# Two norms behind an MLP folded into the next projection's input and eviction, and the squares of the norm before it taken group by group

## What is computed

```python
# end of first_block
h2 = modulate(rmsnorm(x, norm2_g), sh2, sc2)            # h * (1 + sc2) + sh2
x = x + gt2 * (square(relu(h2 @ w_mlp_in)) @ w_mlp_out)  # 2048 -> 8192 -> 2048
x = rmsnorm(x, final_norm_g)
# start of second_block
h = rms_norm(x, norm_mix_pre)
u = h @ w_in                                             # 2048 -> 4352
...                                                      # convolutions and pooling on u, then @ w_out
x = x + rms_norm(y, norm_mix_post)                       # x here is the output of the first block
```

## Time and profile before

| | |
|---|---|
| median of 3 runs | 2858.72 us (2858.38 to 2859.18) |
| the profiled execution, its own time | 2861.59 us |
| its span, first to last instruction | 2859.5 us |
| mean granted TensorE clock in it | 0.969 |
| TensorE busy | 2675.6 us, 94% |
| VectorE busy | 1665.1 us, 58% |
| ScalarE busy | 1158.2 us, 41% |

### The profile page before, as it was taken

The page is one execution under the profiler, slowest core; times in us unless marked ns, Lnnn a source line. Parts: engine busy times, 40 slices in busy tenths (PEclk is TensorE's granted clock), DMA queues, the critical chain, the costliest instruction groups (busy, mean ns, idle before and its releaser), DMA issues.

```text
span 2859.5 us, 45648 instructions
## 1 busy us (share of the span) xinstructions
PE 2675.6 (94%) x20456; PEld 2552.4 (89%) x20456; DVE 1665.1 (58%) x1955; ACT 1158.2 (41%) x1266; POOL 10.6 (0%) x23
## 2 busy tenths in 40 slices
PE   6899999999989999999999799849699999999996
PEld 3488898899989999999999699839599999999996
DVE  4266666387767545455454457954566546654664
ACT  3222555343335434344343343323444434443442
POOL 0000000000000000000000000000000000000000
PEclk9899999999999999999999899969799999999998
DMA  9766565487765655555555244415155555555451
GB/s 375 306 234 229 199 220 192 162 297 273 293 235 215 225 180 184 186 179 190 177 185 184 103 148 154 153 51 188 55 181 181 188 181 188 177 186 183 177 192 45
DMA packets 76211, 546.91 MB, mean 191 GB/s; under 512 B 8720, under 2 KB 8848, under 8 KB 11120
## 3 DMA queue, kind: packets, MB, share of 16 engines
q1 hardware_dynamic: 73424, 533.53, 51.5%
q0 software_dynamic: 2304, 9.96, 0.9%
q10 hardware_dynamic: 288, 0.50, 0.1%
HBM read 538.72 MB, written 5.24 MB: 190 GB/s over the span
## 4 chain that ended last, share of the span: by engine, by line
PE 86%; DVE 8%; DMA 2%; ACT 2%; issue 1%; SPq 0%; POOL 0%; ACTq 0%; DVEq 0%
PE acc L264 24%; PE acc L266 24%; PE acc L268 24%; DVE cacc L1178 2%; PE mp L450 2%; DVE wlo L232 2%; DMA raw<-in_w_mod 2%; PE acc L284 2%; PE acc L285 1%; PE acc L286 1%; PE mp L286 1%; PE mp L284 1%; PE mp L285 1%; PE mp L333 1%; DVE macc L377 1%
## 5 line engine op out<-in xcount | busy, mean ns | idle before, releaser
L232 DVE TENSOR_TENSOR wlo<-raw,whi 128x1024 fp32r<-128x1024 f32 x813 | 984.2, 1223 | 875.3 <-ACT whi L222 873.1
L222 ACT ACTIVATE whi<-raw 128x1024 fp32r<-128x1024 f32 x813 | 853.6, 1058 | 1347.7 <-PE acc L268 1153.4
L264 PE MATMUL acc<-hh,whi 128*128 128x256 f32 x3616 | 1034.5, 286 | 37.0 <-issue 23.7
L266 PE MATMUL acc<-hl,whi 128*128 128x256 f32 x3616 | 1025.6, 284 | 0.0
L268 PE MATMUL acc<-hh,wlo 128*128 128x256 f32 x3616 | 1025.4, 284 | 0.0
L264 PEld LDWEIGHTS acc<-hh,whi 128*128 128x128 f32 x3616 | 695.9, 192 | 48.9 <-issue 39.2
L266 PEld LDWEIGHTS acc<-hl,whi 128*128 128x128 f32 x3616 | 696.2, 193 | 1.2 <-issue 1.0
L268 PEld LDWEIGHTS acc<-hh,wlo 128*128 128x128 f32 x3616 | 695.8, 192 | 0.0
L264 PE MATMUL acc<-mh,whi 128*128 128x256 f32 x2240 | 631.4, 282 | 16.5 <-DVE ml L1262 15.1
L268 PE MATMUL acc<-mh,wlo 128*128 128x256 f32 x2240 | 633.6, 283 | 0.0
L266 PE MATMUL acc<-ml,whi 128*128 128x256 f32 x2240 | 633.6, 283 | 0.0
(11 more groups left out here) (242 smaller groups left out, 1706.6 us busy)
## 6 DMA issues: line engine op xcount, KB each, us to landing
raw<-in_w_in SPq DMA_DIRECT2D x98, 1024.0 KB, 4.8
raw<-in_w_mod SPq DMA_DIRECT2D x96, 1024.0 KB, 5.0
raw<-in_w_up SPq DMA_DIRECT2D x88, 1024.0 KB, 4.8
raw<-in_w_mlp_in SPq DMA_DIRECT2D x64, 1024.0 KB, 4.8
raw<-in_w_mlp_out SPq DMA_DIRECT2D x64, 1024.0 KB, 4.7
raw<-in_w_down SPq DMA_DIRECT2D x44, 1024.0 KB, 4.7
raw<-in_w_out SPq DMA_DIRECT2D x32, 1024.0 KB, 4.8
raw<-in_w_fourier_out SPq DMA_DIRECT2D x8, 1024.0 KB, 4.9
```

Of the source, the lines that this page charges most:

```text
L222: nc.scalar.activation(whi[:, r, :], raw_slot(k)[:, 2 * GC * j:2 * GC * (j + 1)], ACT.Copy)\
L232: nc.vector.tensor_tensor(wlo[:, r, :], raw_slot(k)[:, 2 * GC * j:2 * GC * (j + 1)], whi[:, r, :].bitcast(f32), ALU.subtract).then_inc(S[" ...
L264: nc.tensor.matmul(dst, whi[:, r, cols], hi[:, kt, :], start=begin, stop=False, skip_group_check=True)
L266: nc.tensor.matmul(dst, whi[:, r, cols], lo[:, kt, :], start=False, stop=False, skip_group_check=True)
```

## The change

**norm2.** The squares of quad g are taken behind the eviction of output group g, by ScalarE. VectorE adds the squares of quads 1 and 2 onto those of quad 0, one addition each in groups 2 and 3 (`x2_add`). TensorE sums that total (four matmuls) and behind it the squares of quad 3 (four more). The jobs of the apply are five: two of two tiles, then three of four (`N2_JOBS`), and TensorE waits for them piece by piece (`n2_ready`).

**The two norms behind the MLP.** With f the final norm's weight, m the mix norm's, r1 and r2 the factors per token, h is x * (f * m) * (r1 * r2), and the mean square that r2 needs is r1 * r1 * mean((x * f)^2). So ScalarE writes `hh` as x scaled by `gg` = f * m behind the eviction of each output group of the last MLP chunk, VectorE writes `hl` (`mix_lo`), both without the factors; ScalarE takes the squares of x and of x * f of the same quad (`mix_quad`), VectorE adds them up (`mix_sums`). TensorE goes from the MLP's last group into `w_in_2`, and does the two sums by ones, eight matmuls, in front of the fourth quad of channel tiles of its first group (`u_ready`). Both roots are taken during that group, and r1 * r2 goes in at the eviction of every group of `w_in_2` (`mix_evict`, in place of the copies). x itself gets its f * r1 later, 16 instructions spread over groups 2 to 4.

Removed: `norm_squares`, `norm_root`, `norm_sums`, `norm_rstd` of three norms (2, 3 and 4), L1140, L1143, the four jobs behind them. The other norms are only renumbered. The diff, cut to its core:

```diff
@@ helpers
+        N2_JOBS = [(0, 2), (2, 2), (4, 4), (8, 4), (12, 4)]
+        LO_MIX = 8 + len(N2_JOBS)
+        def ones_sum(pe, dst, part, begin, end):
+            for t in range(4):
+                last = nc.tensor.matmul(dst, ones[:, :], part[:, t * NT:(t + 1) * NT],
+                                        start=begin and t == 0, stop=end and t == 3)
+            return last
...
@@ scalar
             for g in range(0, 4):
                 C(st)
-            all_read(act, F_OUT)
-            norm_squares(act, 2, xT2)
-            norm_root(act, 2, mp[0])
+                i = 1 - g % 2
+                act.wait_ge(acc_free[i], F_FILL[i] + 6 + g // 2 + 1)
+                if g >= 2:
+                    act.wait_ge(S["x2_add"], g - 1)
+                nc.scalar.activation(tiles(tmp[:, min(g, 1), :]), xT2[:, 4 * g:4 * g + 4, :], ACT.Square)\
+                    .then_inc(S["x2_sq"], 1)
+            act.wait_ge(S["x2_ps"], 1)
+            nc.scalar.activation(root[:, :], mp[0][:, 0:NT], ACT.Sqrt, bias=eps[:, 0:1], scale=1.0 / D)\
+                .then_inc(S["x2_rt"], 1)
...
+            act.wait_ge(S["lo_ok"], LO_MIX)
+            def mix_quad(g):
+                act.wait_ge(acc_free[g % 2], F_MLP[g % 2] - 1 + g // 2)
+                for t in range(4):
+                    kt = 4 * g + t
+                    last = nc.scalar.activation(hh[:, kt, :], xT2[:, kt, :], ACT.Copy, scale=gg[:, kt:kt + 1])
+                last.then_inc(S["u_hi"], 1)
+                if g >= 2:
+                    act.wait_ge(S["x4_add"], 2 * g - 2)
+                nc.scalar.activation(tiles(tmp[:, min(g, 1), :]), xT2[:, 4 * g:4 * g + 4, :], ACT.Square)
+                for t in range(4):
+                    kt = 4 * g + t
+                    last = nc.scalar.activation((sqb if g else stage)[:, t * NT:(t + 1) * NT], xT2[:, kt, :],
+                                                ACT.Square, scale=pcol("final_norm_g", kt))
+                last.then_inc(S["x4_sq"], 1)
...
                 for g in range(4):
                     C(st)
-            all_read(act, F_MLP)
...
+                    if c == MLP_CHUNKS - 1:
+                        mix_quad(g)
+            C(st, 6)
+            act.wait_ge(S["x4_ps"], 1)
+            nc.scalar.activation(root[:, :], mp[0][:, 0:NT], ACT.Sqrt, bias=eps[:, 0:1], scale=1.0 / D)\
+                .then_inc(S["x4_rt"], 1)
+            act.wait_ge(S["x4_s"], 1)
+            nc.scalar.activation(root[:, :], tmp[:, 1, 0:NT], ACT.Sqrt, bias=eps[:, 0:1], scale=1.0 / D)\
+                .then_inc(S["x4_rt"], 1)
+            C(st, 2)
+            for b in range(3):
+                C(st)
@@ vector
             for g in range(4):
                 if g:
-                    C()
+                    C(2)
+                    if g >= 2:
+                        sum_add("x2_add", "x2_sq", g - 1, tmp[:, 0, :], tmp[:, 1, :])
+                    C(6)
...
+            dve.wait_ge(S["x2_rt"], 1)
+            own(nc.vector.reciprocal(rstd[:, 0, :], root[:, :]))
+            apply_dve(dve, 8, 0, [(xT2, hh, hl, a, n) for a, n in N2_JOBS])
+            def mix_lo(g):
+                dve.wait_ge(S["u_hi"], g + 1)
+                for t in range(4):
+                    kt = 4 * g + t
+                    last = nc.vector.scalar_tensor_tensor(hl[:, kt, :], xT2[:, kt, :], gg[:, kt:kt + 1],
+                                                          hh[:, kt, :].bitcast(f32), ALU.mult, ALU.subtract)
+                last.then_inc(S["u_lo"], 1)
+            def mix_sums(g):
+                if g:
+                    sum_add("x4_add", "x4_sq", g, tmp[:, 0, :], tmp[:, 1, :])
+                    sum_add("x4_add", "x4_sq", g, stage[:, :], sqb)
...
+                    if c == MLP_CHUNKS - 1 and g:
+                        C(2)
+                        mix_lo(g - 1)
+                        C(2)
+                        mix_sums(g - 1)
+                        C(4)
...
-            norm_rstd(dve, 3)
...
+            C(1)
+            mix_lo(3)
+            C(1)
+            mix_sums(3)
+            C(4)
+            dve.wait_ge(S["x4_rt"], 1)
+            own(nc.vector.reciprocal(rstd[:, 0, :], root[:, :]))
+            own(nc.vector.tensor_tensor(tmp[:, 1, 0:NT], mp[0][:, GC:GC + NT], rstd[:, 0, :], ALU.mult))
+            nc.vector.tensor_tensor(tmp[:, 1, 0:NT], tmp[:, 1, 0:NT], rstd[:, 0, :], ALU.mult)\
+                .then_inc(S["x4_s"], 1)
+            dve.wait_ge(S["x4_rt"], 2)
+            own(nc.vector.reciprocal(rstd[:, 1, :], root[:, :]))
+            own(nc.vector.tensor_tensor(rstd[:, 1, :], rstd[:, 1, :], rstd[:, 0, :], ALU.mult))
+            C(2)
+            def mix_evict(i, dst, n=4):
+                group_done(dve, st)
+                nc.vector.tensor_tensor(dst, tiles(acc[i][:, 0:n * NT]), rbc(1, n), ALU.mult)\
+                    .then_inc(acc_free[i], 1)
...
+                    if g + b:
+                        C(4)
+                        for kt in range(16 * (2 * g + b - 1) // 3, 16 * (2 * g + b) // 3):
+                            nc.vector.scalar_tensor_tensor(xT2[:, kt, :], xT2[:, kt, :], pcol("final_norm_g", kt),
+                                                           rstd[:, 0, :], ALU.mult, ALU.mult).then_inc(S["x1_ok"], 1)
+                        C(4)
+                    mix_evict(b, uT[:, 3 * TA + 8 * g + 4 * b:3 * TA + 8 * g + 4 * b + 4, :])
@@ tensor
-            norm_sums(pe, 2, mp[0])
+            pe.wait_ge(S["x2_add"], 2)
+            ones_sum(pe, mp[0][:, 0:NT], tmp[:, 0, :], True, False)
+            pe.wait_ge(S["x2_sq"], 4)
+            ones_sum(pe, mp[0][:, 0:NT], tmp[:, 1, :], False, True).then_inc(S["x2_ps"], 1)
+            def n2_ready(k0):
+                pe.wait_ge(S["lo_ok"], 9 + (k0 // 2 if k0 < 4 else 1 + k0 // 4))
...
-            norm_sums(pe, 3, mp[0])
-            pe.wait_ge(S["rt_ok"], 4)
-            norm_sums(pe, 4, mp[0])
+            def u_ready(q):
+                pe.wait_ge(S["u_lo"], q + 1)
+                if q == 3:
+                    pe.wait_ge(S["x4_add"], 6)
+                    ones_sum(pe, mp[0][:, 0:NT], tmp[:, 0, :], True, True)
+                    ones_sum(pe, mp[0][:, GC:GC + NT], stage[:, :], True, True).then_inc(S["x4_ps"], 1)
```

More of the change, by code:

```diff
@@ L178, in build @@
             st_ok sm_ok dec_ok o_ok oss_ok ort_ok ons_ok oT_ps ot_ok ohi_ok olo_ok p_ps p_sb y_ps yhi_ok ylo_ok
+            x2_sq x2_add x2_ps x2_rt gg_ok u_hi u_lo x4_sq x4_add x4_ps x4_rt x4_s r1_ok x1_ok
             mt_ok mhi_ok mlo_ok x_back relu_ok rsq_ok hhi_ok hid_ok
@@ L295, in acc_wait, with mm_feature @@
             st.f[i] += evictions
-        def mm_feature(pe, st, i, hi, lo, frees, nkt=KT, w=GC, ready=None, free=None):
+        def mm_feature(pe, st, i, hi, lo, frees, nkt=KT, w=GC, ready=None, free=None, each=None):
             if free:
@@ L306, in mm_feature @@
                     ready(k0 // 4)
+                if each:
+                    each(k0)
                 feature_piece(pe, st, i, hi, lo, k0, nkt, w)
@@ L504, in apply_act @@
                     act.wait_ge(S["lo_ok"], n - 1)
-                for t in range(4):
-                    kt = 4 * q + t
+                for t in range(cnt):
+                    kt = a + t
                     part = tmp[:, n % 2, t * NT:(t + 1) * NT]
@@ L511, in apply_act @@
                 act.wait_ge(S["t2_ok"], n + 1)
-                nc.scalar.activation(hi[:, 4 * q:4 * q + 4, :], tiles(tmp[:, n % 2, :]), ACT.Copy)\
+                nc.scalar.activation(hi[:, a:a + cnt, :], tiles(tmp[:, n % 2, 0:cnt * NT]), ACT.Copy)\
                     .then_inc(S["hi_ok"], 1)
@@ L830, in _ @@
             all_read(act, F_OUT2)
[L831 to L837, removed]
+            norm_squares(act, 2, yT)
+            norm_root(act, 2, mp[0])
+            act.wait_ge(S["vt_ok"], 4)
+            norm_squares(act, 3, xT2)
+            norm_root(act, 3, mp[0])
+            apply_act(act, LO_MIX, [(hh, None, lambda kt: pcol("norm_ffn_pre_2", kt), None, 4 * q, 4)
+                                    for q in range(4)])
+            act.wait_ge(S["lo_ok"], LO_MIX + 4)
             def ffn_pair(st, c, p, n):
@@ L1111, in _ @@
                                            ALU.add, ALU.mult).then_inc(S["mod_b"], 1)
[L1112 to L1113 removed]
+            nc.vector.tensor_tensor(gg[:, :], pcol("final_norm_g", 0, KT), pcol("norm_mix_pre_2", 0, KT),
+                                    ALU.mult).then_inc(S["gg_ok"], 1)
+            dve.wait_ge(S["x2_rt"], 1)
[12 more added lines that the diff above has]
+                    sum_add("x4_add", "x4_sq", g, stage[:, :], sqb)
             for c in range(0, MLP_CHUNKS):
@@ L1134, in _ @@
                     add_scaled(g % 2, 4 * g, 3 * KT).then_inc(acc_free[g % 2], 1)
-            norm_rstd(dve, 3)
[L1137 to L1143, removed]
-                                                   pcol("final_norm_g", 4 * q + t), None, ALU.mult)
-                last.then_inc(S["vt_ok"], 1)
@@ L1146, in _ @@
```

(4 more changed lines are left out.)

96 lines of the change are left out of this document (42 added, 54 removed).

## The result

| | before | after |
|---|---|---|
| median, us | 2858.95 (2858.38 to 2862.04, 4 runs) | 2796.86 (2794.68 to 2798.17, 4 runs) |
| ratio | | 0.978, 95% interval 0.9763 to 0.9797 |
| profiled execution, its own time | 2861.59 | 2798.17 |
| its span | 2859.5 | 2796.4 |
| mean granted TensorE clock | 0.969 | 0.975 |

What follows compares the result with a forecast made beforehand. TensorE's matmul pace was taken as the bound (VectorE in the convolution stretch), with gains only in pauses: 42.1 behind the MLP plus 8.0 at norm2 is 50.1, from 2858.72 to 2808.6 us; range 2804 to 2817.

Steps and rivals of the forecast that it cites:

- That pace changes only with the number of matmuls: Filled stretches: TensorE starts one matmul per 0.120 us, 2.88 us per piece, so only pauses can be won.
- The seam: Pause behind the MLP: 43.9 us removed, plus 1.6 of low clock, less 3.4 for eight added matmuls: 42.1 us gained.
- norm2: First pause: TensorE restarts at 852.0 to 853.8 instead of 863.06, then stalls 2.0 us; gain 8.0 us (7.2 to 9.0).
- Rival 2: Ends of MLP groups: ScalarE's new block takes 9 us for 4.5, fifth piece late; 15 us lost, 2823.5; chance 0.05.
- Rival 3: First group of w_in_2: TensorE waits for VectorE's last addition before the sums; 5 us late gives 2812; no chance given.
- the spare time at the fifth piece: Behind the MLP's last group: its wlo is ready at T+10.7, TensorE wants it at T+11.5, 0.8 us spare.
- the other reading of the tier table: Evictions in the convolution stretch: products slower than copies would cost up to 3 us; forecast took no cost.
- Rival 4: Without the pause, TensorE's clock falls from lack of rest: 2.2 us more per piece, 2883 us; chance 0.03.
- 2 us either way: Allowance in the forecast's own range, because the clock's rises and falls behind the later pauses shift.

Runs made afterwards that it cites:

- Kernel 1: The kernel before with 64 unused bytes per partition where the changed kernel has gg, no instruction changed: 2845.49 us, ratio 0.9947.
- kernel 2: The changed kernel with gg put behind all other buffers, so every other buffer has its address of before: 2811.41 us, ratio 0.9825.
- kernel 3: kernel 2 with norm2 put back in its old form (four jobs of four tiles, all 16 matmuls by ones in a row): 2816.86 us, ratio 0.9848.
- kernel 6: The changed kernel with 32 unused bytes in front of hh and 64 in front of the buffers with mh: 2791.78 us, ratio 0.9756.
- kernel 7: The changed kernel with 96 unused bytes in front of hh and 64 in front of the buffers with mh: 2800.80 us, ratio 0.9788.
- Kernel 8: The changed kernel with 32 unused bytes in front of whi, not hh, and 96 in front of the buffers with mh: 2807.83 us, ratio 0.9812.
- kernel 10: The changed kernel run once more, unaltered, on the same chip as a rerun of kernel 4: 2797.80 us, ratio 0.9783.
- kernel 5: kernel 4 with 32 unused bytes in front of hh and 96 in front of the buffers with mh: 2762.90 us, ratio 0.9653.
- kernel 9: The kernel before with 32 unused bytes in front of hh and 160 in front of the buffers with mh, no instruction changed: 2816.64 us, ratio 0.9845.
- kernel 4: The changed kernel with the fifth piece of the first MLP group converted before the last job of norm2's apply: 2790.13 us, ratio 0.9762.

## Why the prediction was wrong

**The step that failed** is none of the two sums but the sentence before them: "One piece is 24 matmuls, 2.88 us [...] That pace changes only with the number of matmuls." It changed by 2% where not one matmul was added or removed. The first line of the whole diff, left out of the core shown ahead of the prediction, is a buffer of 64 bytes, `gg = sb("gg", [P, KT])`. It moved `mh`, `ml` and all behind them, and I gave that line no cost, not even an unknown one. Kernel 1 prices it alone at 14.5 us; kernel 2 takes it away from the change and lands at 2811.4, 2.8 above the forecast and inside the range. That it lands so near is in part luck: the seam gave 1.1 us more than forecast and norm2 2.5 less.

| term | forecast | measured | from |
|---|---|---|---|
| seam, pause and low clock less eight matmuls | 42.1 | 42.4 in the trace, 43.2 by medians | first row below, kernel 3 |
| norm2 | 8.0 (7.2 to 9.0) | 5.5 by medians, 4.2 to 8.5 in traces | kernels 3 and 2, traces below |
| displacement by gg | none | 14.5 | kernel 1 |
| sum | 50.1 | 63.2, against 62.1 measured | |

**The seam** came as forecast in every step. From the end of the MLP to the eviction of `w_in_2`'s second group it was 1699.47 - 1605.37 = 94.1 us before and 1640.69 - 1588.94 = 51.75 after, 42.4 less. The two rows, of the kernel before and the changed one:

```profile
1699.47 1.22 DVE L1152 COPY uT<-acc 128x1024 f32<-128x1024 f32 x1
```

```profile
1640.69 1.22 DVE L1217 TENSOR_TENSOR uT<-acc,rstd 128x1024 f32<-128x1024 f32 x1
```

They also show that the product in the eviction costs what the copy did, 1.22 us, so the other reading of the tier table in the Trainium skill ("VectorE: DVE Perf Modes", The perf-mode tier table), a copy faster than `tensor_tensor`, did not come true in float32. Rivals 2 and 3 did not come: the spare time at the fifth piece was 1.1 us.

**norm2** was mis-sized, the lesser error. The times of its steps held; one thing the sum left out is what the clock does with a short stall. Behind the 2.8 us the stretch 866.2 to 870 had clock 0.59: 20 matmuls in 3.8 us, where 20 x 0.120 = 2.4 us would do. That is 1.4 us. The Trainium skill ("TensorE: Matmul & The Clock Gate", What's actually happening) says the default is the slow clock and activity releases it; here the clock fell behind the stalls of 2.8, 2.5, 3.0 and 2.7 us (the changed kernel, kernels 2, 6 and 7) and not behind those of 2.25 and 2.28 us (kernels 8 and 10). Measured from the last rounding before the pause to the fixed place L392 or L397: 48.6 us before and 46.6 in kernel 3, with the same instructions; 42.4 and 40.1 in the changed kernel's two traces, 42.0 in kernel 2. Kernel 1, the old norm2 too, has 47.3, and kernels 7 and 8, the new one, 42.3 and 40.1. So the same instructions vary by some 2 us there, and the low clock covers a different part of them in each trace. The gain is between 4.2 and 8.5 us, and 6.1 between the means of the three old and the five new. My 8.0 is in that span, toward its end; the trace that I had measured it against is the longest of the three.

**Rival 4** (the clock held low without the pause) did not come: PEclk is 1.00 in the stretch over the seam and behind it.

**What it cost to be wrong.** The range had 2 us either way for all that the sum did not name. A layout change was visible in the whole diff, and the trace of before even held a hint: the matmuls on `mh` there alternated 121.5, 118.5 and 120 ns by line, where those on `hh` had 120 each. Equal means hid it.

## What to carry to other kernels

A buffer added in the middle of the others is a change of its own: run the kernel before with the same number of unused bytes, or put the new buffer last, before you explain the difference by the instructions. Where a kernel is bound by back-to-back matmuls, it is worth a run to try the distance between stationary and moving operand: it took 32 and 160 bytes here to gain 46 us of 2862, nearly as much as the change's instructions gave (48.6, kernel 2). That other types, shapes or kernels answer alike is not shown. And a stall that a change creates costs more than its length when the clock falls behind it; here one piece of work moved ahead of the last job took it from 2.8 to 0.3 us.

## What the runs showed that I had not expected

**The pitch of split matmuls depends on where the two operands lie to each other.** The weights are a 128x128 block of `whi` or `wlo`, the moving operand a 128x256 tile of `hh`, `hl`, `mh` or `ml`, all fp32r. The traces hold no addresses. If the buffers lie one behind the other in the order of the program, each rounded up to 32 bytes, which I take and which fits all kernels, the distance from the weights, modulo 128 bytes, and the pitch in the MLP's stretches is:

| moving minus weights, modulo 128 | pitch, ns | where |
|---|---|---|
| 0 | 120.0 | `hh` before and after, `mh` in 6, both in 8 |
| 32 | 116.7 to 117.8 | `mh` after (117.3), `hh` in 6 (117.8), both in 5 and 9 (116.7) |
| 64 | 117.8 | `mh` in 7 |
| 96 | 120.0, uneven by line | `mh` before, `hh` in 7 |

Kernel 8 rules out that the moving operand's own address decides alone; that the distance does is the simplest reading that fits, with the test named there still to be made. Nor is the distance all of it: `hh` lies at the same place in kernels 5, 6 and 9 and has 116.7, 117.8 and 116.7, while `mh` lies elsewhere in 6. What in the chip makes it so is not shown. Nor is why `mh` in the changed kernel has 118.8 in the output projection and 117.3 in the MLP.

**It adds to the rest, to within a few us.** 14.5 for one pair of operands, 27.2 to 31.2 for the rest of it (kernel 5 against 4), 45.8 for all of it in the kernel before. In the MLP's stretches conversions and transfers had room for the faster pace: in kernel 5 DMA is at 0.53 of its time and VectorE at 21 of 40 us. Not all of it arrives: 17568 of these matmuls by 3.3 ns are an estimated 58 us, from the pitches 120.0 and 116.7, and kernel 9 gained 45.8. In part other engines bound the pace, as VectorE does in the convolution stretch; the parts were not told apart.

**The best version** is kernel 5, 2762.9 us: the change, the early piece, and 128 unused bytes. It beats both kernels, the one before by 101 us on the same chip, and the changed one by some 34 to 39 (the difference of the medians, and of the gains, 101.1 against 62.1; they were not run side by side).
